# The filter stage of a one-core Hyena and attention step: adaLN sums moved into unit slots, tap sums from GpSimd to VectorE

## The reference, cut to what matters

```python
def hyena_filter_spectrum(L, p):
    ...
    z = jnp.concatenate([t, jnp.cos(f * w), -jnp.sin(f * w)], axis=-1)
    fq = p['hy_freq'].astype(F32)
    h = jnp.sin(fq[0] * (z @ p['hy_f_w1'].astype(F32) + p['hy_f_b1'].astype(F32)))
    h = jnp.sin(fq[1] * (h @ p['hy_f_w2'].astype(F32) + p['hy_f_b2'].astype(F32)))
    h = (h @ p['hy_f_w3'].astype(F32)).reshape(L, 2, HY_ORDER, D_HY)
    ...
    h = h * jnp.exp(-t * deltas)[:, None, None, :]
    h_f, h_b = h[:, 0], h[:, 1]
    h_full = jnp.concatenate([h_f, jnp.zeros((1, HY_ORDER, D_HY), F32), h_b[1:][::-1]], axis=0)
    h_full = h_full / (jnp.sum(jnp.abs(h_full), axis=0, keepdims=True) + NORM_EPS)
    return jnp.fft.rfft(h_full, axis=0)

def trunk_layer(x, cond, p, lam, lam_init, rope, ctx_k, ctx_v):
    mod = jax.nn.silu(cond) @ p['w_ada'] + p['b_ada']
    shift, scale, gate = jnp.split(mod[:, None, :], 3, axis=-1)
    h = rms_norm(x, p['norm_g']) * (1.0 + scale) + shift
    ...
```

## Time and profile before

| what | us |
|---|---|
| runs before (three) | 3654.05, 3655.55, 3656.89 |
| median | 3655.55 |
| the profiled execution's own time | 3656.49 |
| its span in the trace | 3654.8 |
| filter stage up to the first spectrum of unit 0 | 141.5 |
| unit 0 | 93.5 |
| unit 1 | 76.6 |
| unit 2 | 74.3 |
| unit 3, with the end of the stage | 52.3 |
| the rest: two layers | 3216.6 |

### The profile page before, as it was taken

One profiled execution on the slowest core, in us unless ns is written; L12 is line 12 of the kernel. 1 busy time (PEld: TensorE's weight loads), 2 busy tenths in 40 slices (PEclk: granted clock), 3 DMA queues, 4 the chain that ended last, 5 costly groups with the idle time before them and its releaser, 6 DMA issues. The chain is left out here.

```text
span 3654.8 us, 48036 instructions
## 1 busy us (share of the span) xinstructions
PE 3290.3 (90%) x18198; PEld 3065.0 (84%) x18198; DVE 1842.4 (50%) x2353; ACT 1080.1 (30%) x1714; POOL 793.4 (22%) x393
## 2 busy tenths in 40 slices
PE   2588799899999999988999699999999999889999
PEld 2366599889889999966899697988989999867999
DVE  7667342444544673268562332544543763288451
ACT  2244342334434112122221332443442122122211
POOL 3223021121221111122122221122121121122223
PEclk9988999999999999999999899999999999999999
DMA  6465634424422443366544423442423443465534
GB/s 209 155 201 188 211 130 129 115 89 123 128 87 89 155 155 131 126 234 219 175 154 144 170 88 116 125 122 94 121 93 112 154 144 138 145 222 202 188 130 161
DMA packets 222805, 536.29 MB, mean 147 GB/s; under 512 B 37748, under 2 KB 95861, under 8 KB 221206
## 3 DMA queue, kind: packets, MB, share of 16 engines
q1 hardware_dynamic: 215670, 507.95, 41.5%
q10 hardware_dynamic: 6912, 25.17, 2.7%
HBM read 397.80 MB, written 162.28 MB: 153 GB/s over the span
## 5 line engine op out<-in xcount | busy, mean ns | idle before, releaser
L2150 PE MATMUL ps<-hh,w_high 128*128 128x384 f32 x1152 | 409.5, 356 | 5.5 <-ACT attn_fout L2301 4.4
L2150 PE MATMUL ps<-hh,w_low 128*128 128x384 f32 x1152 | 390.6, 339 | 0.0
L2150 PE MATMUL ps<-hl,w_high 128*128 128x384 f32 x1152 | 389.1, 338 | 0.0
L1371 PE MATMUL ps<-hh,w_high 128*128 128x384 f32 x1344 | 310.7, 339 | 7.2 <-PEq L116 7.2
L1371 PE MATMUL ps<-hl,w_high 128*128 128x384 f32 x1344 | 306.7, 336 | 0.0
L1371 PE MATMUL ps<-hh,w_low 128*128 128x384 f32 x1344 | 306.4, 335 | 0.0
L2480 DVE TENSOR_TENSOR attn_wl<-ps,attn_wh 128x512 fp32r<-128x512 f32 (+2 forms) x200 | 117.4, 587 | 290.5 <-ACT attn_wh L2337 290.5
L2460 DVE TENSOR_REDUCE attn_nmax<-ps 128x1 f32<-128x1280 f32 x144 | 195.4, 1357 | 135.5 <-PE ps L2173 135.4
L1371 PEld LDWEIGHTS ps<-hh,w_high 128*128 128x128 f32 x1344 | 240.2, 189 | 11.7 <-POOLq L1470 7.8
L2327 ACT ACTIVATE low<-ps,attn_nmax 128x1280 f32<-128x1280 f32 x144 | 176.4, 1225 | 233.6 <-DVE attn_nmax L2460 233.6
L1371 PEld LDWEIGHTS ps<-hh,w_low 128*128 128x128 f32 x1344 | 240.8, 189 | 0.0
(11 more groups left out here) (300 smaller groups left out, 7302.2 us busy)
## 6 DMA issues: line engine op xcount, KB each, us to landing
tables<-in_dft_conv SPq DMA_DIRECT2D x64, 512.0 KB, 4.3
gates<-attn_fout SPq DMA_DIRECT2D x144, 192.0 KB, 2.8
branch_gate<-gates SPq DMA_DIRECT2D x48, 576.0 KB, 4.1
w_raw<-in_w_mg ACTq DMA_DIRECT2D x48, 512.0 KB, 4.0
mixin_grow<-in_w_ada SPq DMA_DIRECT2D x48, 512.0 KB, 3.6
conv_dh<-tables SPq DMA_DIRECT2D x96, 256.0 KB, 2.9
conv_dl<-tables SPq DMA_DIRECT2D x96, 256.0 KB, 3.4
aux<-qk SPq DMA_DIRECT2D x64, 288.0 KB, 6.1
```

Source lines behind the costliest of these rows:

```text
L1371: last = pe.matmul(dst, w[:, b, k, :], x[:, k, cols], start=(k == 0 and n == 0), stop=(k == KD - 1 and n == 2))
L2150: last = pe.matmul(ps[:, X_BANK, 0:CH], w[:, j % 2, k, :], x[:, k, (c % 3) * CH:(c % 3 + 1) * CH], start=(k == 0 and n == 0), stop=(k == K ...
```

## The change

- The adaLN numbers of layer 0 leave the opening. They are made in sixteen slots of units 1 to 3 (`ADA_SLOTS`), on DVE at the end of a step. There is one buffer for the piece of `w_ada_first`; SP loads it two steps ahead and waits for the slot before. The condition vectors are loaded anew in units 1 to 3 at s = 4, behind a wait for the landing of the store from `hpout`, which shares their place; ACT applies Silu at s = 6. The later `mixers_in` loads the condition vectors itself and applies Silu.
- `both_of` moves from POOL to DVE, right behind the second `decayed` of its block.
- In the opening of unit 0 a block's folds come right behind its taps; turns, absolute values and splits follow block by block too.
- Of the copies of the hidden numbers, the two that fill layer 0 are awaited at the first taps, the high ones issued by SP, the low ones by ACT. The copies for layer 1 are awaited in unit 2.
- All eight pieces of x are loaded first, each to a place of its own; six of the squares stand between the two sines.
- The folds' scratch `once` shares memory with w3, so w3 of the next unit is loaded behind the last fold that uses it.

The diff, cut to its core:

```diff
-xs = (both[:, 2, 1], taps[:, 0, 0], taps[:, 0, 1], taps[:, 1, 0], taps[:, 1, 1], spare, taps[:, 0, 0], taps[:, 0, 1])
-condb = both[:, 3, :, 0:D_MODEL]
-once = [araw[:].rearrange("p a n -> p (a n)")[:, 3 * BR + i * (FOLD + 1):3 * BR + (i + 1) * (FOLD + 1)] for i in range(2)]
-waste = hout[:].rearrange("p a n -> p (a n)")
+xs = (both[:, 2, 1], both[:, 3, 0], both[:, 3, 1], taps[:, 0, 0], taps[:, 0, 1], taps[:, 1, 0], taps[:, 1, 1], spare)
+once = [w3_once[:, i * (FOLD + 1):(i + 1) * (FOLD + 1)] for i in range(2)]
+condb, ada_in = araw[:, 0:2], araw[:, 2]
+waste = draw[:].rearrange("p a k c -> p (a k c)")
+ADA_SLOTS = {1: (8, 10, 12, 14, 16), 2: (8, 10, 12, 14, 16), 3: (7, 9, 11, 13, 15, 16)}
+ada_at = {key: i for i, key in enumerate((n, s) for n, slots in ADA_SLOTS.items() for s in slots)}
...
+                sp.wait_ge(S["fold"], 2 * folded(n - 1, CT - 1, 2) + 2)
...
         def load_ada(i):
-            if i >= 3:
-                sp.wait_ge(S["ada"], 2 * (i - 2))
-            sp.dma_start(araw[:, i % 3], A["w_ada_first"][i]).then_inc(s_ain[i % 3], 16)
+            if i:
+                sp.wait_ge(S["ada"], 2 * i)
+            sp.dma_start(ada_in, A["w_ada_first"][i]).then_inc(S["ain"], 16)
...
-        sp.dma_start(condb, A["cond"].to_broadcast([P, 2, D_MODEL])).then_inc(S["cond"], 16)
-        for i in range(2):
-            load_ada(i)
-        for k in range(6):
+        for k in range(KD):
             load_x(k)
         for u in range(2):
             load_decay(u)
+        for m in range(2):
+            load_matrix(m)
-        for m in range(2):
-            load_matrix(m)
-        sp.wait_ge(S["scond"], 1)
-        sp.dma_start(cond_kept, condb).then_inc(S["cst"], 16)
-        for k in range(6, KD):
-            load_x(k)
-        for i in range(3, 5):
-            load_ada(i)
...
         sp.wait_ge(S["hi"], 1)
-        sp.wait_ge(S["lo"], 1)
-        for p in range(2):
-            for half in range(2):
-                sp.dma_start(hid[0][p][half * HY_FFN:(half + 1) * HY_FFN].bitcast(F32),
-                             hid[1][p][0:HY_FFN].bitcast(F32)).then_inc(S["dup"], 16)
-        sp.wait_ge(S["dup"], 64)
+        for half in range(2):
+            sp.dma_start(hid[0][0][half * HY_FFN:(half + 1) * HY_FFN].bitcast(F32),
+                         hid[1][0][0:HY_FFN].bitcast(F32)).then_inc(S["duph"], 16)
+        for u in range(2, CT):
+            load_decay(u)
+        sp.wait_ge(S["duph"], 32)
+        sp.wait_ge(S["dupl"], 32)
         for p in range(2):
             sp.dma_start(hid[1][p][0:HY_FFN].bitcast(F32), hid[1][p][HY_FFN:P].bitcast(F32)
                          ).then_inc(S["dup"], 16)
-        for i in range(5, 9):
-            load_ada(i)
-        for u in range(2, CT):
-            load_decay(u)
-            for i in range(9 + 2 * (u - 2), 11 + 2 * (u - 2)):
-                load_ada(i)
-        for i in range(13, NA):
-            load_ada(i)
         for u in range(CT, CT + 2):
             load_decay(u)
         sp.dma_start(x_state[0], A["x"]).then_inc(S["x"], 16)
...
+                if s == 4 and n in ADA_SLOTS:
+                    sp.wait_ge(S["hpst"], 16 * (n + 1))
+                    sp.dma_start(condb, A["cond"].to_broadcast([P, 2, D_MODEL])).then_inc(S["cond"], 16)
+                if (n, s + 2) in ada_at:
+                    load_ada(ada_at[n, s + 2])
...
-                pe.wait_ge(S["ang"], 2)
-                if n:
+                if n == 0:
+                    pe.wait_ge(S["ang"], 2)
+                    pe.wait_ge(S["duph"], 32)
+                    pe.wait_ge(S["dupl"], 32)
+                else:
                     pe.wait_ge(S["hpo"], n)
+                if n == 2:
+                    pe.wait_ge(S["dup"], 32)
...
+            if m == 1:
+                pe.wait_ge(S["begun"], 1)
...
+        hidden_to_taps(0, 0, 0)
         for ct in range(CT):
-            for d in range(2):
-                hidden_to_taps(0, ct, d)
-        for ct in range(CT):
+            hidden_to_taps(0, ct, 1)
+            if ct + 1 < CT:
+                hidden_to_taps(0, ct + 1, 0)
             for f in (0, 2, 4):
                 turn(0, ct, f)
...
-        w3_low(0)
         dve.wait_ge(S["hi"], 1)
         dve.tensor_tensor(hid[1][1][:], h2, hid[1][0][:].bitcast(F32), ALU.subtract).then_inc(S["lo"], 1)
+        w3_low(0)
...
-                else:
+                elif u == 0:
                     dve.wait_ge(S["xadd"], KD - 1)
...
+        def both_of(n, ct):
+            u = n * CT + ct
+            t = taps[:, u % 2]
+            dve.wait_ge(S["taps"], 2 * u + 2)
+            dve.memset(t[:, 1, 0:TS + 1:TS], 0.0).then_inc(S["zero"], 1)
+            dve.wait_ge(S["zero"], u + 1)
+            if n:
+                dve.wait_ge(S["fold"], 2 * folded(n - 1, ct, 3) + 2)
+                dve.wait_ge(S["tr"], group(n - 1, ct, 4) + 1)
+            elif ct < 3:
+                dve.wait_ge(S["sin"], 2)
+                dve.wait_ge(S["lo"], 1)
+                if ct == 2:
+                    dve.wait_ge(S["ssm"], 1)
+            dve.tensor_tensor(both[:, ct, 0], t[:, 0], t[:, 1], ALU.add).then_inc(S["both"], 1)
+            dve.tensor_tensor(both[:, ct, 1], t[:, 0], t[:, 1], ALU.subtract).then_inc(S["both"], 1)
...
+            dve.wait_ge(S["w3l"], n + 1)
...
-        for i in range(2, 6):
-            modulation(i)
         for m in range(2):
             matrix_low(m)
+        decayed(0, 0, 0)
         for ct in range(CT):
-            for d in range(2):
-                decayed(0, ct, d)
-                modulation(6 + 2 * ct + d)
-        for i in range(14, NA):
-            modulation(i)
-        dve.wait_ge(S["ada"], 2 * NA)
-        chain(dve.memset(once[1][:, 0:1], 0.0))
-        for ct in range(CT):
+            decayed(0, ct, 1)
+            both_of(0, ct)
+            if ct:
+                for f in (2, 4):
+                    low_part(0, ct - 1, f)
             for f in (0, 2):
                 folds(0, ct, f)
-                if f == 2:
-                    low_part(0, ct, 0)
-                    low_part(0, ct, 2)
-                    low_part(0, ct, 4)
+            if ct + 1 < CT:
+                decayed(0, ct + 1, 0)
+            low_part(0, ct, 0)
+        for f in (2, 4):
+            low_part(0, CT - 1, f)
         norms(0)
         dve.wait_ge(S["ssm"], 1)
-        dve.tensor_copy(sums[:], ps[:, 5, 0:NT // P])
+        dve.tensor_copy(sums[:], ps[:, 1, 0:NT // P]).then_inc(S["begun"], 1)
...
+        def modulation(n, i):
+            dve.wait_ge(S["scond"], n)
+            dve.wait_ge(S["ain"], 16 * (i + 1))
+            for st in range(2):
+                if 2 * i + st:
+                    dve.wait_ge(S["ada"], 2 * i + st)
+                dve.tensor_tensor_reduce(waste, ada_in, condb[:, st], 1.0, 0.0, ALU.mult, ALU.add,
+                                         modn[:, i, st:st + 1]).then_inc(S["ada"], 1)
...
                         decayed(n + 1, (s - 2) // 2, s % 2)
+                        if s % 2:
+                            both_of(n + 1, (s - 3) // 2)
                     for ct, f in even_groups(s):
                         low_part(n + 1, ct, f)
                     if s == 15:
                         norms(n + 1)
+                if (n, s) in ada_at:
+                    modulation(n, ada_at[n, s])
+                if n + 1 < NU:
                     if s == 16:
                         folds(n + 1, 0, 1)
...
-        act.wait_ge(S["cond"], 16)
-        nc.scalar.activation(condb, condb, ACT.Silu).then_inc(S["scond"], 1)
...
             if i == 1:
-                squares((2, 3, 4))
+                squares(range(2, KD))
...
         nc.scalar.copy(hid[1][0][:], h2).then_inc(S["hi"], 1)
+        act.wait_ge(S["lo"], 1)
+        for half in range(2):
+            act.dma_start(hid[0][1][half * HY_FFN:(half + 1) * HY_FFN].bitcast(F32), hid[1][1][0:HY_FFN].bitcast(F32)
+                          ).then_inc(S["dupl"], 16)
...
         w3_high(0)
-        squares((5, 6, 7))
...
             act.wait_ge(S["H"], m + 1)
-            if m == 0:
-                act.wait_ge(S["ada"], 2 * NA)
...
-        for ct in range(CT):
             for f in (0, 2, 4):
                 high_part(0, ct, f)
...
+                        act.wait_ge(S["ada"], 2 * sum(len(ADA_SLOTS[p]) for p in ADA_SLOTS if p < n))
...
+                if s == 6 and n in ADA_SLOTS:
+                    act.wait_ge(S["cond"], 16 * n)
+                    nc.scalar.activation(condb, condb, ACT.Silu).then_inc(S["scond"], 1)
```

More of the change, by code:

```diff
@@ L179, in build @@
         modn = keep("modn", [P, 2 * KD, 2])
-        cond_kept = scratch("cond_kept", [P, 2, D_MODEL])
         sums = keep("sums", [P, NT // P])
-        filters(nc, A, ps, modn, cond_kept, ident, ones, sums, x_state, H_dram, Hp_dram, hinv, split)
+        filters(nc, A, ps, modn, ident, ones, sums, x_state, H_dram, Hp_dram, hinv, split)
         with nc.Fori(0, DEPTH) as l, nc.sbuf_tensor("low", [P, CT, NT], F32) as low, \
```

(9 more changed lines are left out.)

57 lines of the change are left out of this document (10 added, 47 removed).

## The result

The changed kernel took 3674.59 us (median of 5 runs, 3670.39 to 3679.41), the kernel before 3655.55 (3654.05 to 3657.94): ratio 1.0055, 95% interval 1.0044 to 1.0067. That is 19 us slower; forecast were 6.5 us faster, and the time lies outside the range of 3637 to 3665.

What follows compares the result with a forecast made beforehand. VectorE was taken to bound the opening, with TensorE busy 64 of 75 us in units 1 and 2. Terms -21.5 - 1 + 6.4 + 5.4 + 4 = -6.7 against 3656.5 gave 3649.8, stated as 3649; range 3637 to 3665.

Steps and rivals of the forecast that it cites:

- opening, to the first spectrum out: Filter stage's start until ACT takes the first spectrum out: 21.5 us shorter, bounds -14 and -29.
- unit 1: Filter stage, unit 1: 6.4 us longer with adaLN slots, tap sums and a Silu table load, bounds 0 and +12.
- unit 2: Filter stage, unit 2: 5.4 us longer, from +3.2 for VectorE and +2.2 for SP, bounds 0 and +12.
- unit 3: Filter stage, unit 3: 4 us longer, VectorE having room, bounds 0 and +9.
- The lock of the second reduction: Opening: VectorE's range reduction operations each wait for POOL's running add, so the reduction ends at about 47.4.
- the block chain: Opening, taps and folds: each block a VectorE chain with one hand-over to PE, 13.4 us; first spectrum could start at 112.6.
- the third matrix behind x_state: Opening's end: the matrix lands at about 124 behind that copy, so 21.5 of the 28.9 us arrive.
- VectorE's term: Units 1 and 2: added tap sums and adaLN pairs cost +3.2 us, between 0 and +9.5.
- SP's term: Units 1 and 2: stores and parts standing behind an adaLN load's wait cost +2.2 us.
- the condition: Unit 3: 1,024 KB issued ahead of step 7's parts makes PE wait some 2.7 us.
- the bytes: Unit 3 from step 7 on: 256 KB more a step on the mean, ten steps costing 1 to 2 us.
- The rival "slower": Units 1 to 3: SP's list waits, PE lacks parts at most slots; +12, +12, +9 us, 3666 us; chance 0.17.

Runs made afterwards that it cites:

- condition once: Changed kernel with the condition loaded once, in unit 1, and its Silu kept in the place of layer 0's hidden numbers; all pieces and pairs stay: 3671.0 us.
- three buffers: Kernel with the condition loaded once, given three buffers for the adaLN pieces in place of one: 3640.6 us, ratio 0.9968 to the kernel before.
- pairs alone: Changed kernel with all sixteen pairs on VectorE but only one piece of the weights and one load of the condition: 3638.8 us.
- the kernel without adaLN: Changed kernel without layer 0's adaLN numbers (no pieces, condition, Silu or pairs in the filter stage; set to zero), tap sums still on VectorE: 3631.2 us.

## Why the prediction was wrong, step by step

| step | forecast | measured | what it rests on |
|---|---|---|---|
| opening, to the first spectrum out | -21.5 | -23.0 | 146.5 and 123.5 |
| unit 0 | -1 | 0.0 | 88.2 and 88.2 |
| unit 1 | +6.4 | +12.5 | 77.0 and 89.5 |
| unit 2 | +5.4 | +10.3 | 74.3 and 84.6 |
| unit 3 | +4 | +19.5 | 48.3 and 67.8 |

**The opening was right, with its mechanism.** The lock of the second reduction, the block chain and the third matrix behind x_state all came as worked out. That the first spectrum came at 112.7 against 112.6 is partly luck: the first product was 2.0 us late, and the blocks took 12.5 to 13.1 in place of 13.4. What the prediction did not see is that the new order's share in this was next to nothing: taking the sums out gave 22.5 us alone, and the rest of the gain stood behind the copy of x.

For the reduction the prediction had left open which operations wait for POOL. The row at 32.36 decides: an operation with one SBUF input took 3.05 beside an add and takes 0.76 without one. The Trainium skill, in "SBUF — State Buffer", section "SBUF: two separate sides", says that VectorE takes the shared pair not only with two SBUF inputs but also in a two-port mode, and that the loser blocks for a whole instruction; the 3.05 agrees with that, though no row shows which mode the operation ran in. A row of the kernel before could have told it: the same kind of operation started beside the last of three adds, which ended at 36.24, and took 1.65.

```profile
35.20 1.65 DVE L226 TENSOR_SCALAR fspec_both<-fspec_both 128x1152 f32<-128x1152 f32 x1
```

**VectorE's term lay within its bounds in unit 2, and its work was free in unit 3.** For sums and pairs +3.2 was taken against the kernel before; sums and pairs without the loads gave 75.5 - 74.3 = +1.2 in unit 2 and -0.2 in unit 3. In unit 1 the same kernel stands at +8.7, and what of that is VectorE's stays open. The Silu there was put at 0.9 us and takes 1.9.

**SP's term failed.** The prediction put +2.2 in units 1 and 2 for the stores and parts that stand behind an adaLN load's wait, and nothing in unit 3, where it counted the condition (2.7) and the bytes (1 to 2). Measured by taking the hold away (one buffer to three, condition once in both): 6.0 in unit 1, 10.1 in unit 2, 15.0 in unit 3, 31 us in all, with 30 us in the medians. ACT's waits for stores fall with it, to 10.0, 6.1 and 5.1 us. The bytes were put at 1 to 2; with three buffers, where unit 3 loads no condition, it is still 4.0 longer than before, and how much of that the bytes are is not shown. The condition was not told apart from no change in the medians (3671.0, 3668.2 to 3673.4, against 3674.6).

The rival "slower" named the right list and what holds it, though it looked for the loss in PE's waits for parts alone, with a price of 33 us for the three units (42.3 came), and it was given 0.17 because "a part needs 3 us and has two steps, 7 us, to come". This is the sentence that failed. The two steps are counted from when SP issues, and the wait decides when SP issues. A piece for step s + 2 is asked for at step s and waits for the pair of step s, the last thing VectorE does in that step; that pair itself waits for the piece that was asked for just before it (4.22). So at each slot SP comes down to VectorE's pace. In units 1 and 2 VectorE in its turn waits for ACT as well as for pieces, as a low part needs the high part that ACT makes. In unit 2 of the changed kernel (idle time at the end of each line):

```profile
L707 DVE CUSTOM_DVE_ANT_0 fspec_draw<-fspec_araw 128x1024 f32<-128x1024 f32 x11 | 13.4, 1220 | 8.1 <-DMA fspec_araw<-in_w_ada_first 7.9
L656 DVE TENSOR_TENSOR fspec_xl<-ps,fspec_xh 128x512 fp32r<-128x512 f32 x16 | 10.8, 685 | 16.0 <-ACT fspec_xh L795 15.9
```

ACT's list holds the copies of the spectra too, and these wait for SP's stores (23.1 us in this unit). So SP waits for VectorE, VectorE for ACT, and ACT for SP. The sentence counts the lead of a part, which has three places; a store has two, and the prediction never counted its lead. In unit 3 the first pair stands behind the last low part; from then on piece and pair alone make the loop of 6.6 to 6.8 us, longer than two steps. Either way the lead is used up at the first slot and does not come back. The longest gap costs a second time in slow matmuls: 6.5 of the 19.5 us of unit 3 are PE's busy time, with the granted clock at 0.50, the lower of its two levels, from 414 to 422.

What stays open: what unit 1 pays above unit 2 with pairs alone (9.6 against 4.6 over the kernel without adaLN), and what in the last 4 to 6 us of units 1 and 2 is VectorE's. A kernel with one buffer whose pieces are issued from a list of their own, which would part the held list from the loop altogether, was not run.

## What to carry to other kernels

A load that waits for its own consumer, in the list that also issues everyone else's loads, brings that whole list down to the consumer's pace: count the lead of a transfer from when its list can reach it, not from the step it is written in. Give such a load more buffers (three in place of one gave 30 us here), or write it behind the transfers that are due first (18 us). And where a long opening is shortened, look for the one large transfer that was hidden in it and for what stands behind it in its queue. When a unit is measured to its last result, look also at what still runs behind it before the next phase can start.

## What the runs showed of the hardware

- VectorE's single-input operation on 128x1152 in SBUF waited for POOL's add as a two-input one does: 3.05 us beside it and 0.76 without, against 3.67 (11.01 / 3) and 1.38.
- A Fourier matrix of 128x256, asked for 7.7 us behind a copy of 4.6 MB on the same queue (111.25 after 103.56), landed at 123.2, behind the copy (121.4). With the copy issued on another queue, at 52.6, and over by 71.4, the matrix was there 3.5 us after it was asked for (110.74 to 114.2).
- In unit 3 PE waited 5.9 us and then ran from 414 to 422 at a granted clock of 0.50; over the unit the clock was 0.90 against 1.00, and PE's busy time 51.7 against 45.2 for the same matmuls.
